# Feed-forward output products as block products in one series with the input half, and the last two tiles half by half

## The reference

```
def swiglu_ffn(h, w_in, w_out):
    g, u = jnp.split(h @ w_in, [D_FF], axis=-1)
    return (jax.nn.silu(g) * u) @ w_out
```

## Time and profile before

| what | value |
|---|---|
| median of three runs | 1286.08 us |
| the profiled execution, its own time | 1286.95 us |
| its span, first to last instruction | 1285.1 us |
| TensorE busy | 1260.3 us, 98% |
| VectorE busy | 785.1 us, 61% |
| ScalarE busy | 576.6 us, 45% |
| GpSimd busy | 427.0 us, 33% |
| matmuls | 9438 |

### The profile page before, as it was taken

How to read it: one execution, slowest core, us unless ns; L and a number is a source line. 1 busy time by engine, 2 the same in 40 slices (tenths; PEclk the granted TensorE clock), 3 DMA queues, 4 the chain that set the end, 5 groups by cost and what they waited for, 6 DMA issues and landing times.

```text
span 1285.1 us, 23305 instructions
## 1 busy us (share of the span) xinstructions
PE 1260.3 (98%) x9438; PEld 1211.6 (94%) x9438; DVE 785.1 (61%) x1361; ACT 576.6 (45%) x1037; POOL 427.0 (33%) x250
## 2 busy tenths in 40 slices
PE   9999999999999999999999999999999999999997
PEld 8888999999999999999889999899999999999996
DVE  5776757972277316658446787678961466317655
ACT  5565545562277415743023454225461366317631
POOL 1000033423322332236565544464323322232150
PEclk9999999999999999999999999999999999999998
DMA  9411122273277425743232332223263277416632
GB/s 328 162 34 50 51 67 77 73 163 91 70 177 160 129 83 122 164 117 117 77 104 87 116 125 97 86 78 119 81 150 92 86 159 166 124 66 155 143 106 74
DMA packets 50569, 145.43 MB, mean 113 GB/s; under 512 B 7088, under 2 KB 11120, under 8 KB 49024
## 3 DMA queue, kind: packets, MB, share of 16 engines
q1 hardware_dynamic: 33968, 107.30, 25.9%
q0 software_dynamic: 12960, 23.60, 11.0%
q10 hardware_dynamic: 3536, 13.05, 2.8%
HBM read 136.46 MB, written 9.44 MB: 114 GB/s over the span
## 4 chain that ended last, share of the span: by engine, by line
PE 83%; DVE 6%; DMA 4%; issue 3%; ACT 2%; POOL 1%; SPq 1%; ACTq 0%; DVEq 0%
PE ps L689 26%; PE ps L691 25%; PE ps L690 25%; DMA wlo<-w_blocks_in 1%; PE ps L819 1%; PE ps L866 1%; DMA more_lo<-w_blocks_in 1%; POOL wlo L640 1%; PE ps L842 1%; DMA sinks<-sinks_in 1%; PE ps L1150 1%; PE ps L1157 1%; DMA wst<-w_blocks_in 1%; DVE S L1874 1%; DVE more_lo L1578 0%
## 5 line engine op out<-in xcount | busy, mean ns | idle before, releaser
L640 POOL TENSOR_TENSOR wlo<-wst,whi 128x1024 fp32r<-128x1024 f32 x100 | 249.3, 2493 | 346.4 <-ACT whi L2126 343.7
L689 PE MATMUL ps<-hid,whi 128*128 128x288 f32 x704 | 208.9, 297 | 2.8 <-POOL wlo L640 2.8
L689 PE MATMUL ps<-xhi,whi 128*128 128x288 f32 x688 | 209.0, 304 | 1.1 <-DVE wlo L1371 0.7
L690 PE MATMUL ps<-hid,whi 128*128 128x288 f32 x704 | 208.2, 296 | 0.0
L691 PE MATMUL ps<-hid,wlo 128*128 128x288 f32 x704 | 208.0, 295 | 0.0
L690 PE MATMUL ps<-xlo,whi 128*128 128x288 f32 x688 | 202.9, 295 | 0.0
L691 PE MATMUL ps<-xhi,wlo 128*128 128x288 f32 x688 | 202.2, 294 | 0.0
L2126 ACT ACTIVATE whi<-wst 128x1024 fp32r<-128x1024 f32 x66 | 69.8, 1058 | 168.4 <-PE ps L691 168.4
L689 PEld LDWEIGHTS ps<-xhi,whi 128*128 128x128 f32 x688 | 129.0, 187 | 9.6 <-issue 8.3
L689 PEld LDWEIGHTS ps<-hid,whi 128*128 128x128 f32 x704 | 132.6, 188 | 4.3 <-POOL wlo L640 4.2
L691 PEld LDWEIGHTS ps<-hid,wlo 128*128 128x128 f32 x704 | 132.3, 188 | 0.0
(11 more groups left out here) (288 smaller groups left out, 3045.7 us busy)
## 6 DMA issues: line engine op xcount, KB each, us to landing
wst<-w_blocks_in SPq DMA_DIRECT2D x188, 512.0 KB, 3.5
wlo<-w_blocks_in POOLq DMA_DIRECT2D x60, 256.0 KB, 4.4
more_lo<-w_blocks_in POOLq DMA_DIRECT2D x30, 256.0 KB, 5.1
S<-s_in ACTq DMA_DIRECT2D x4, 1024.0 KB, 5.0
s_sample_out<-S ACTq DMA_DIRECT2D x4, 1024.0 KB, 4.4
y_out<-x SPq DMA_DIRECT2D x16, 144.0 KB, 1.8
bias<-bias_in SPq DMA_DIRECT2D x1, 2048.0 KB, 11.1
x<-x_in SPq DMA_DIRECT2D x4, 288.0 KB, 7.0
```

What stands on the lines that cost most here:

```text
L640: nc.gpsimd.tensor_tensor(lo, wst[:, slot, :], raw(hi), ALU.subtract).then_inc(w_split, 1)
L689: mm(out, stat[0], mov[0], start=start, stop=False, skip_group_check=skip)
L690: mm(out, stat[0], mov[1], start=False, stop=False, skip_group_check=skip)
```

## The change

- The output half of the first two phases goes by seven products as well. A phase becomes four units `("out", phase, i)`, each for two x tiles; the operands are the hidden tiles of the phase (4 + 4) as 2x2 blocks and the sums T1 to T4 of those. They stand in one series with the input units: in 4..7, out, in 8..15, out, in 16..21. The third phase stays plain.
- The hidden tiles 0 to 15 are therefore stored in halves, and T1 to T4 of them are formed on DVE (`hidden_sum`), their high parts on ACT (`sum_high`), their low parts by subtractions of 128x288 on POOL (`hidden_low`).
- In the first output unit of a phase, P2 comes last. The results of an output unit are added to x by DVE (`top`, `corner`, `left_x`).
- The blocks d2 to d7 of a layer (`AHEAD`) get their low part by a negated copy on ACT and an adding DMA of 128x1024 (`direct_high`, `direct_low`) in place of the subtraction on POOL. They use three places in turn.
- A22 of every unit, and A11 and A12 of all but the first of a layer, come by adding DMA; ACT's copy of P1 and the high part of A11 change places with S4 and S3 in the first unit.
- In layer 1 the last two x tiles do the third phase half by half, in place of the last one doing phases 1 and 2.

```diff
 ORDER, IN_AT, DOWN_AT = block_order()
-B_LAST = NBLK - 2
-SEVEN = {IN_AT[l][f] + u: (l, f) for l in range(2) for f in range(N_DIRECT, FC) for u in range(2)}
+AHEAD = range(2, 2 * N_DIRECT)
+UNITS = ([("in", f) for f in range(N_DIRECT, 8)] + [("out", 0, i) for i in range(4)] +
+         [("in", f) for f in range(8, 16)] + [("out", 1, i) for i in range(4)] + [("in", f) for f in range(16, FC)])
+def blocks_of(l, u):
+    return (IN_AT[l][u[1]], IN_AT[l][u[1]] + 1) if u[0] == "in" else tuple(DOWN_AT[l][u[1]][2 * u[2]:2 * u[2] + 2])
+SEVEN = {n: (l, u) for l in range(2) for u in UNITS for n in blocks_of(l, u)}
...
-NOT_OWN = [n for n0, n1, own in HI_PARTS if not own for n in range(n0, n1) if n in COUNT] + [NBLK - 1]
+MOVED = {B_F1[l] + d: (l, d) for l in range(2) for d in AHEAD}
...
@@ -462,69 +485,80 @@
         def split_of(n):
+            if n in MOVED:
+                l, d = MOVED[n]
+                return direct_moved[d % 3], 16 * (2 * l + d // 3 + (d % 3 == 2))
...
         def ring(n):
-            return (o1hi[:, :], o1lo[:, :]) if n == B_O1 + 2 else (whi[:, n % RING, :], wlo[:, n % RING, :])
+            if n == B_O1 + 2:
+                return o1hi[:, :], o1lo[:, :]
+            if n in MOVED:
+                l, d = MOVED[n]
+                if d % 3 == 2:
+                    return third_hi[:, :], third_lo[:, :]
+                n = B_F1[l] + d % 3
...
+            def direct_low(l, d):
+                n = B_F1[l] + d
+                pool.wait_ge(direct_neg, len(AHEAD) * l + d - 1)
+                pool.dma_start(ring(n)[1], io["w_blocks"][ORDER[n]], accum_op=ALU.add).then_inc(split_of(n)[0], 16)
...
+                j = f % 4
+                pool.wait_ge(ht_hi[op], turn_of(l, f))
+                if op == "T2":
+                    pool.wait_ge(ht_lo["T1"], turn_of(l, f))
+                nc.gpsimd.tensor_tensor(htlo[op][:, j, :], htraw[op][:, j, :], raw(hthi[op][:, j, :]), ALU.subtract
+                                        ).then_inc(ht_lo[op], 1)
             def ffn(l):
...
+                quarter_low("A11", l, UNITS[0])
+                quarter_low("A12", l, UNITS[0])
+                prev = None
+                for u, nxt in zip(UNITS, UNITS[1:] + [None]):
+                    f = prev[1] if in_halves(prev) else None
...
+                        split(DOWN_AT[l][2][0])
+                    if f is not None and first_half(f):
+                        hidden_low(l, "T1", f)
+                    quarter_low("A22", l, u)
+                    quarter_low("A12", l, nxt)
+                    if f is not None and not first_half(f):
+                        hidden_low(l, "T4", f)
+                    if u in UNITS[0:2]:
...
+                    prev = u
+                for n in DOWN_AT[l][2][1:]:
                     split(n)
...
+                def seven(u, before):
+                    o, a = ordinal(l, u), bank_of(u)
+                    last, fresh_out = u == UNITS[-1], u[0] == "out" and u[2] == 0
                     if o > 2:
-                        pe.wait_ge(hidden_done, o - 2)
-                    else:
...
+                        pe.wait_ge(seven_read, o - 2)
+                    pe.wait_ge(std_done, k + 1)
+                    product(1, "A11", "B11", u, a, True)
                     if o > 1:
-                        pe.wait_ge(gate_half, 2 * o - 2)
-                    product(5, "S1", "T1", f, 7, True)
-                    if f == pairs_of(phase_of(f))[-1]:
-                        product(2, "A12", "B21", f, 6, True)
+                        pe.wait_ge(top_read, 2 * o - 2)
+                    product(5, "S1", "T1", u, 7, True)
+                    if last:
+                        product(2, "A12", "B21", u, 6, True)
                     if before is not None:
                         left_up(before)
                     pe.wait_ge(copied[1], o)
-                    product(6, "S2", "T2", f, a, False)
-                    if f != pairs_of(phase_of(f))[-1]:
-                        product(2, "A12", "B21", f, 6, True)
+                    product(6, "S2", "T2", u, a, False)
+                    if not last and not fresh_out:
+                        product(2, "A12", "B21", u, 6, True)
                     pe.wait_ge(copied[5], o)
-                    product(3, "S4", "B22", f, 7, False)
+                    product(3, "S4", "B22", u, 7, False)
                     pe.wait_ge(copied[6], o)
-                    product(7, "S3", "T3", f, a, False)
...
             def last_down():
...
-                    for c in range(KC, FC):
-                        n, w = B_LAST + c // KC - 1, slice(c % KC * P, (c % KC + 1) * P)
-                        if a == 0 and c == 2 * KC:
-                            pe.wait_ge(last_split, 1)
-                        hi, lo = hidden_tile(c)
-                        ins = three(ps[:, 2 + a, 0:H], (whi[:, n % RING, w], wlo[:, n % RING, w]),
-                                    (hi[:, s], lo[:, s]), c == KC, c == FC - 1)
-                        if a == 1 and c == KC + 5:
-                            last_sums(0)
-                        if a == 1 and c == KC + 10:
-                            spread(0, 6)
-                    ins.then_inc(last_half, 1)
+                    for i, m in enumerate(LAST_TILES):
+                        n = DOWN_AT[1][2][m]
+                        if a == 0:
+                            pe.wait_ge(*split_of(n))
+                            pe.wait_ge(*added(1, m - 2))
+                        for c in range(f1 - f0):
+                            hi, lo = hidden_tile(f0 + c)
+                            w = slice(c * P, (c + 1) * P)
+                            ins = three(ps[:, 2 * i + a, 0:H], (whi[:, n % RING, w], wlo[:, n % RING, w]),
+                                        (hi[:, s], lo[:, s]), c == 0, c == f1 - f0 - 1)
+                            if a == 1 and i == 0 and c == 3:
...
+                    if op == "T1":
+                        if f >= N_DIRECT:
+                            dve.wait_ge(seven_read, ordinal(l, ("in", f)))
+                        else:
+                            dve.wait_ge(u_read[l], f + 1)
+                        a, b = htraw["T3"][:, j, :], left
+                    elif op == "T4":
+                        dve.wait_ge(ht_lo["T2"], turn_of(l, f))
+                        dve.wait_ge(seven_read, ordinal(l, ("in", f)))
+                        a, b = left, htraw["T2"][:, j, :]
+                    elif op == "T2":
+                        dve.wait_ge(ht_lo["T1"], turn_of(l, f))
+                        a, b = right, htraw["T1"][:, j, :]
+                    else:
+                        a, b = right, htraw["T3"][:, j, :]
+                    tt(out, a, b, ALU.subtract).then_inc(ht_sum[op], 1)
...
+                        tt(gs[:, H:N], ps[:, 7, 0:H], kept[:, 2, :], ALU.add).then_inc(top_read, 1)
+                        return
+                    xl, xr = x[:, 2 * u[2], 0:H], x[:, 2 * u[2], H:N]
+                    dve.wait_ge(copied[1], o)
+                    chain.link(tt(xl, xl, kept[:, 0, :], ALU.add))
+                    dve.wait_ge(copied[6], o)
+                    chain.link(tt(xr, xr, kept[:, 2, :], ALU.add))
                     dve.wait_ge(product_done[2], o)
-                    dve.wait_ge(copied[1], o)
-                    tt(gs[:, 0:H], ps[:, 6, 0:H], kept[:, 0, :], ALU.add).then_inc(gate_half, 1)
...
+                        return
+                    xr = x[:, 2 * u[2] + 1, H:N]
+                    chain.link(tt(xr, xr, kept[:, 1, :], ALU.add))
                     dve.wait_ge(product_done[7], o)
-                    dve.wait_ge(copied[5], o)
-                    tt(h32[:, H:N], ps[:, 4 + f % 2, 0:H], kept[:, 1, :], ALU.add).then_inc(up_right, 1)
...
+                    f = u[1]
                     dve.wait_ge(silu_done[l], f + 1)
-                    dve.wait_ge(up_right, ordinal(l, f))
-                    tt(h32[:, H:N], h32[:, H:N], gs[:, H:N], ALU.mult)
...
-                            sum_low("S4", f + 1)
-                            sum_low("S3", f + 1)
-                    left_hidden(fs[-1])
-                    hidden_low(fs[-1])
-                    if l == 0 and ph == 2:
-                        dve.wait_ge(h_lo[0], FC)
-                        nc.vector.memset(raw(shi[:, :, :]), 0.0)
-                        ins = nc.vector.memset(raw(slo[:, :, :]), 0.0)
-                        chain.link(ins)
-                    ms = KC - 1 if l and ph else KC
-                    nxt = PHASES[ph][1]
-                    for m in range(ms):
-                        if ph < 2 and m == ms - 1:
-                            sum_s1(nxt)
-                            sum_s2(nxt)
-                            sum_low("S1", nxt)
-                            sum_s4(nxt)
-                            sum_low("S2", nxt)
-                        down(ph, m)
-                    if ph < 2:
...
+            def last_tile(a, i):
```

(86 more changed lines are left out.)

627 lines of the change are left out of this document (350 added, 277 removed).

## The result

The changed kernel takes **1316.3 us** (median of four runs, 1312.33 to 1318.46), the kernel before 1285.5 beside it: a ratio of 1.024, 95% interval 1.021 to 1.027. It is slower by 31 us where 11.5 us of gain were forecast, and the time lies outside the range given.

A forecast was written before the change was run, and what follows sets the result against it. TensorE's matmul pace was taken to bound the kernel: -25.5 for matmuls and -6 for borders, with added waits of 4.9, 3.2, 4.2, 1.4, 4.8, 1.0 and 0.5, gave -11.5 us, so 1274.5 us, range 1258 to 1283.

The forecast's parts named there:

- item 3: Block d2, once a layer: TensorE waits for the 512 KB DMA, landing after 5.8 us; together +4.9 us, bounds 2 and 7.
- item 5: Units after second-half hidden tiles: POOL's T2 and T3 subtractions delay P1's copy and A11's DMA; +4.2 us, plus 1.4.
- item 4: Units after hidden tiles 8 to 11: short waits for P6's copy and A22's DMA, 8 x 0.4 = +3.2 us.
- the series absorbs it: Rival: a wait in one unit gives slack to the next, only d2 and the end cost; 1260 us, chance 0.28.
- 1, matmuls: Output half of the first two phases: 48 matmuls less in each of four phases, 192 in all, -25.5 us on TensorE.
- 2, borders: Borders of phases: four of six go, with their waits for POOL's subtraction, copies and A quarters; -6 us.
- PE's clock falls at d2: Rival: a pause of 3 us at d2 costs a block at half pace; +6.4 us in all, 1281 us, chance 0.07.
- 6, first output unit: First output unit of a phase, P2 last: P4 waits for x by the corner; +1.2 each, +4.8 us in all.
- 8, first unit of a layer: First unit of a layer: DVE's top halves stand ahead of S2 and T4; +0.5 each, +1.0 us in all.
- 9, the end: Kernel's end: 12 more small sums on TensorE, five tiles for DVE to scale instead of two; +0.5 us, bounds -1 and 2.
- The slower rival: A11's DMA, issued 3 us later behind POOL's subtractions in 16 units, becomes the bound; 1298 us, chance 0.10.
- wrong if PE waits 20 us or more in the series: Sign against the forecast: TensorE waiting 20 us or more in the seven-product series, or under 3, would make it wrong.

The follow-up runs named there:

- all7: all4 plus three order edits: ACT copies P1 first and S3's high part goes earlier behind second halves, DVE's corner earlier there and in the first unit: 1272.2 us.
- all8: all7 with A11's high part and DMA, in input units, ahead of the high parts and subtractions of T2 and T3: 1265.6 us, ratio 0.984.
- last_order: Changed kernel with A22's high part and DMA put ahead of the third phase's first block split in a layer's last unit: 1309.7 us, ratio 1.019.
- d2_sub: Changed kernel with block d2's low part by POOL's subtraction again, in place of negated copy and 512 KB DMA: 1301.1 us, ratio 1.012.
- copy_first: Changed kernel with one edit: behind the second halves ACT copies P1 ahead of the high parts of T2 and T3: 1310.0 us, ratio 1.019.
- t1_late: Changed kernel with T1 of tiles 8 to 11 moved behind A22, P6's copy and S1 on ACT, behind A22's DMA on POOL: 1306.3 us, ratio 1.016.
- corner_first: Changed kernel with DVE doing the corner ahead of the top halves in the first output unit of a phase: 1310.1 us, ratio 1.020.
- all4: Changed kernel with the edits of d2_sub, last_order, t1_late and corner_first together: 1283.4 us, ratio 0.9985.

## Why the prediction was wrong

**The steps that failed.** The removed matmuls came as forecast. The costs were too low in four places: item 3 (the landing of the DMA of 512 KB, 5.8 us for a measured 8.8 to 9.4, and a clock taken as unchanged behind the wait), item 5 (a cost of 0.35 us a unit behind the second halves, measured 1.15), item 4 (a wait priced at its idle time, half of what it takes), and the last unit of a layer, which stood in no item (7.5 us).

**Where the time went.** With the gains as forecast (-25.5 and -6) the new costs would have been 62 us, to come out at the +30.6 of the span; my items 3 to 9 add up to 20. The edits give, one by one: d2 15.8, the last unit 7.5, T1 11.0, corner 7.0, then 11.0 (all7) and 7.2 (all8) on top of the four together. Put in one on top of another they give back 51.8 us. The tail, which none of them takes out, costs 1.4. All8 is at -21.2 us in span, 4.3 short of the 25.5 that TensorE's work shrank by, and 1.4 of it is the tail. Its time, 1265.6 us, is near the 1260 of the rival that I called "the series absorbs it", but that rival is not borne out: nothing was absorbed in the orders as made, and it took eight edits to get there, seven of them of order only.

**1, matmuls:** right in kind and size, -25.5 us of busy time in all8. The kernel as changed is busy for 15.3 us more than all8 with the same 9258 matmuls; some 9 us of that are the lower clock, by the matmuls that ran at 0.50 behind the two waits at d2 and the two for A22 (2.6, 2, 1.6 and 3.1 us), and the rest may be restarts, which busy time doesn't tell apart. So its span is +30.6 = -25.5 + 15.3 + 40.8 of idle time. **2, borders:** not measured by itself. The waits for POOL's first subtraction went from 3.0 to 1.4 us, and 1.26 of the 1.4 is a new one in the tail; at the two borders that stay they were hidden behind the wait for A22, and last_order brings them back (0.47 each).

**3, block d2: mis-sized by three, and with the wrong remainder.** Forecast +4.9 with bounds 2 and 7; 15.8 (d2_sub). By its own rows the term was 0.3 short (213.3 less 210.27 is 3.0, not 2.7), which is nothing beside the rest. Two things failed. The landing: I took 5.8 us since "the packets double in size and not in number"; it was 8.8 in the median and 9.4 here, twice the 4.4 of half the bytes. The packets did double in size and not in number (144 for each such DMA before and after, by the queue's 12960 for 90 and 23616 for 164), and that didn't help. My upper bound of 6.7 took for the second half the queue's mean time for 256 KB, 1.57 us, with the engines to itself. That it shares them here with the block loads and with the transfers of d3 and d4 behind it is what I take for the reason, and no run sets it apart; also the quickest of the four landings of `third_lo` took 7.3. The Trainium skill (DMA: Bandwidth & Descriptors, Anatomy of one DMA) fits such a DMA as 2.0 us plus bytes over 436e3 per us, 2.6 for 256 KB and 3.2 for 512; for these adding DMAs the trace has 4.4 and 8.8, and the measurement decides. The second: the rival "PE's clock falls at d2" had 0.07 and 6.4 us; it came true together with the longer wait, and cost some 4.6 us at d2 in both layers. As a step: a wait of several us was priced by its length.

**4, tiles 8 to 11: waits right, price wrong.** Forecast +0.4 a unit, 3.2 in all; measured 0.48 in rows of idle time and 0.96 in the period, 7.7 in all; of the 11.0 by the edit, 2.8 are not its own. I took a wait's idle time for its cost. In the steady units of before there was no wait; the few waits at its borders could have given the factor, and I didn't lay them against a stretch without.

**5, second halves: mis-sized by three.** Forecast +0.35 a unit; the period is 12.33, +1.15. The first half of the mechanism was right (POOL's subtractions take 0.8 and shut DVE out), and all7 and all8 give back 18.2 us, in the main by taking the copy of P1 and A11's transfer out from behind T2 and T3. The second half, which had 0.25 of the 0.35, was not: in the changed kernel TensorE waits once for A11, 0.3 us, and the landings for `wlo` are at 4.4 as before; what it waits for are the copy of P1 and A22. I had ACT's copy of P1 late by 0.1 and counted neither the restart nor that DVE, once late, stays late through the unit: one addition ran 3.44 us, where I had priced each overlap by itself, and in copy_first, where only the copy's place is another, the longest such addition is 1.91. The Trainium skill (SBUF — State Buffer, SBUF: two separate sides) has an exclusive lock between the two, which whichever starts first holds for its whole instruction; the trace agrees in that DVE's addition ends 0.6 us after POOL's run of three, but its row begins 0.23 us ahead of the first of them, so the order of the starts is not borne out. The lock can pass from one POOL instruction to the next without DVE getting its turn. I had let them "take turns".

**6, first output unit:** P4's wait was forecast at 1.2 and is 1.47; the wait of P6 for its copy (0.89) wasn't in the sum. The corner alone gave 7.0, of which 2.9 are not its own, for 4.8. **7, other output units:** right, no wait in 47 us. **8, first unit of a layer: wrong.** Waits of 1.95 and 2.35 us for a forecast of 0.5 each. I looked at DVE's own order and not at what POOL had queued beside it: in layer 0 two instructions in front of the corner take 1.30 and 1.10 us for 0.69. That is 1.0 of the 1.95; for the rest DVE, hardly ever idle from 262 us on, was late by its own order. **9, the end:** forecast +0.5, measured +1.4 (0.3 to 2.4), within its bounds. The wait is for POOL's subtraction, in front of the first sums; I had counted DVE and TensorE only.

**What was missed altogether: the last unit of a layer,** 7.5 us. The rule to name every queue that an instruction is moved past was applied to the steady unit and not to the exceptions (`if nxt is None`), though both lines stand in the diff.

**The slower rival,** the transfers behind the subtractions, did not come true: it asked for a median landing of 5.1 us or more for A11, and this is 4.4. That the time came out on its side of zero is no credit to it. What decided is the sum of the units behind the second halves and the copies in them (18.2 us given back for 5.6 forecast), one mis-sized DMA (15.8 for 4.9), one missed order (7.5 for nothing) and a factor of two on short waits. The forecast named the alternative itself ("wrong if PE waits 20 us or more in the series"), and it does: the waits for copies, for `more_lo`, for x and for h are 34.9 us. The chance of "faster" was stated 0.03 under the sum of its cases, and was far too high.

**Open.** In all8 ten waits for copies (4.3 us) remain; whether the subtractions of T1 to T4 on another engine than POOL would take them away wasn't tried. How much of the 18.2 us of all7 and all8 belongs to DVE held up less and how much to ACT's order wasn't separated; that the amount of POOL's work is not to blame, the 11.2 us of those units in all8 show. What makes the clock fall behind one wait of some 2.4 us and not behind another is open as well, and it moves the span of single runs by 2 to 3 us.

## What to carry to other kernels

In a stream that has no gaps, count each new wait as its idle time plus a fixed restart (0.24 us here), and a long one (2.6 to 7.3 us here) at up to 3 us more still, since the clock can fall behind it. When a single edit is sized by two spans, look at the stretches that it doesn't touch: 3 of 11 us, and 3 of 7, were not the edit's. When a change lengthens the orders of ACT, DVE and POOL, put first in each queue what TensorE waits for (copies out of its banks, the issue of a transfer), then what has slack, and walk the first and the last unit as carefully as the steady one. A sound idea put in a poor order looks like a bad idea: the same block products gave +31 us and, with eight edits around them, -20.

## What the runs showed of the hardware

- A short wait of TensorE costs 0.24 us beside its row: 12.13 against 11.17 us in a unit with two waits of 0.48 together.
- The granted clock was 0.50 for 5.4 us of matmuls behind a wait of 7.34 us, and 0.92 in the 15 us behind one of 2.82. The length of the wait alone doesn't settle it: behind a wait of 2.35 us at the first unit of layer 1 the changed kernel and copy_first stayed at 1.00, while t1_late (0.91 from 952 to 970 us), last_order, corner_first, d2_sub and all4 fell; behind one of 2.85 us corner_first stayed at 1.00 (571 to 585 us).
- An adding DMA from HBM took 4.4 us for 256 KB and 8.8 for 512 KB (medians, the large ones all in the busy stretches at a layer's start); cut in two the wait for it was 6.6 instead of 7.3 us.
- An addition on DVE with two operands in SBUF that takes 0.69 us alone took 3.44 beside three subtractions on POOL back to back, and none of them took over 1.91 once ACT's copy of P1 stood elsewhere (copy_first).
